# Splitting the first block by token halves, with half 1 computed among the expert gathers of half 0

## The chip, the cores and the metric

The kernel runs on one core of a Trainium2 chip. The metric is the device time of one execution in microseconds. A core has TensorE (PE, with its weight loads shown as PEld), VectorE (DVE), ScalarE (ACT), GpSimd (POOL) and SyncE (SP, which here only issues transfers). Each engine takes its instructions strictly in the order in which the program puts them into its queue.

## The reference, cut to what matters

The input is 256 tokens of width 1024. A first block adds an attention and convolution mixer and then a layer of retrieved experts; a second block (not touched by the change) follows.

```python
h = rmsnorm(x, ln_mix_g) * (1 + sc1) + sh1              # sh, sc, gt: columns of silu(c) @ w_mod + b_mod
q, kc, vc, ksl, vsl, kw, vw, gts, cb, cc, ch = jnp.split(h @ w_in, SPLIT_POINTS, axis=-1)
o_attn = nsa_mixer(...)      # 8 heads of 64: compressed blocks, all selected blocks, window, summed by gates
o_conv = cb * conv3(cc * ch) # causal, 3 taps, 512 channels
mixed = concatenate([rmsnorm(o_attn, norm_attn_g), rmsnorm(o_conv, norm_conv_g)])
x = x + gt1 * (mixed @ w_out)
h2 = rmsnorm(x, ln_ffn_g) * (1 + sc2) + sh2
x = x + gt2 * peer_ffn(h2, peer_wq, peer_keys, peer_u, peer_v)
# peer_ffn, for each token and each of 8 heads: query (2 x 64), scores against 2 x 128 keys, top 16 of each,
# top 16 of the 16 x 16 sums -> 128 experts a token, of 16384; weights g = softmax(top scores);
# act = gelu(h2 . u[e]);  out = sum over e of g * act * v[e]
```

## The kernel before

The tokens are two halves of 128, one token a partition; keys 0 to 127 serve queries of half 0, all 256 those of half 1, since attention is causal. The program is written as queues: `V(...)`, `A(...)`, `PE(...)`, `G(...)` and `SP.dma(...)` append an instruction with the ones that it waits for (`after`), so the order of the Python statements is each engine's order. All of them are issued by one helper, line 87, which is why every row of the profile bears that number. A float32 matmul is two instructions, so 8 accumulated ones count 16.

Weights stream through four slots of `W` (2 MB each, 512 columns) in the order of `plan`; `next_w` takes the next, `done_w` starts the load of the one four further on. PSUM has eight banks, taken in turn by `ps.take()`.

The order of the first block is this. (1) The projections: queries `qT`, the keys and values, the gates, then the three convolution parts (`cbT`, `ccT`, `z`, in six pieces of 32 instructions); behind each of the six, `run_step(2)` issues two of twelve `steps`: window scores, compressed blocks, their scores (`cmp_scores`), transposes (`cmp_turn`) and products (`cmp_add`). GpSimd does six weighted column sums (`mod_sum`) meanwhile. (2) Eight units of window attention, `scores(u)`, `turn_p(u)`, `pv_(u)`, four for each half (`units` holds half, group and kind); the convolution, four `conv_step(j)` over 256 columns, lies among the last. `scores` is matmuls, an add from PSUM, a row maximum (VectorE), four exponentials (ScalarE) and the weighting by sum and gate (VectorE). (3) Column sums, both norms over 256 columns, `mixT`. (4) `attn_mm(0)`, `attn_add(0)`, `queries(0)` (norm, transposes to `hT`, the projection to `qp` in two parts, key scores, transposes back to `tok2`), `attn_mm(1)`, the first two heads of `route(0)`, `attn_add(1)`, `queries(1)`.

Then the gathers begin: a loop over u in 0..255, unit u being one of the 128 chosen experts (u % 128) for each of the 128 tokens of half u // 128.

```python
for u in range(2 * P):
    n, t = fetch(a, q)          # GpSimd: indirect DMA, 128 rows of u and v, 8 KB each, into buffer n of 7
    t_dot[u] = n, V(ttr, ...)   # VectorE: dot product of the u row with tok2, one column of av
    e = combine(u)              # ScalarE: gelu, times gw, diagonal matrix dg; TensorE: dg @ v rows into PSUM
    if routes:
        advance(routes[0], 3)   # VectorE: the next 3 routing instructions
```

The seven buffers `GB` lie over `AR`, the memory of the first stages. A gather waits until TensorE has combined what was in its buffer. `route(a)` is a generator of VectorE instructions (`max`, `match_replace`, `max_index`, sums of candidates, a table lookup by `is_equal`), in groups of two, two and four heads, with one ScalarE exponential a group; `t_idx[a, h]` are the indices of a head, which the fetch of units 16h and on waits for. At u = 64 and 80 `mod_row` sums the weights of the second gate over a row; from u = 128 on the end of half 0 and the first projections of the second block lie among the gathers. Behind the loop comes the rest of the second block.

Of the kernel before, what the change touches and what calls it, by code (L numbers as in the profile page):

```python
# [112 lines left out]
def build(nc, x, cst, oh, pc, cmpw, keysT, rel, rows, ab, w_mod, w_in, w_out, wq, puv,  # L113
          w_in2, wba, wbb, wo2, out, scr):
    ctx = ExitStack()
    with ctx:
# [83 lines left out]
        s_row = dsem("s_row")  # L200
        mixT = sb("mixT", [P, 8, S])
# [13 lines left out]
        cw = ar(4288)[0:64, :]  # L215
        s_cw = dsem("s_cw")
# [73 lines left out]
        def mod_row_sum(r, n, buf, t):  # L290
            b = ps.take()
            t = PE(mm, b.t[:, :], ones, buf, start=True, stop=True, after=b.old + [t, t_in])
            o = rowb[:, r, n * 512:n * 512 + 512]
            b.free = [V(tt_, o, b.t[:, :], o, ADD, after=[t, t_row])]
            return b.free[0]

        def mod_row(r, n):
# [8 lines left out]
            b.free = [V(tt_, o, b.t[:, :], o, ADD, after=[t, t_row])]  # L306
# [9 lines left out]

        junk = sb("junk", [P, D])
# [71 lines left out]
        qT = ar(4 * S).rearrange("p (j t) -> p j t", j=4)  # L389
# [13 lines left out]
        blk = ar(2 * 32 * 30)[0:64, :].rearrange("p (v q g n) -> p v q g n", v=2, q=32, g=2)  # L403
        ksT = ar(S)
        kwT = ar(S)
        vtok = ar(2 * 2 * 128).rearrange("p (a r d) -> p a r d", a=2, r=2)
        gts = ar(48).rearrange("p (a n) -> p a n", a=2)
# [41 lines left out]
        for r in range(4):  # L449
            SP.dma(nc.sync.dma_start, s_row, rowb[:, r, :], rows[r, :].partition_broadcast(P))  # L450
# [48 lines left out]
        Pc = ar(256).rearrange("p (a h n) -> p a h n", a=2, h=8)  # L499
        cst_ = sb("cst_", [P, 2, 8, 2])  # L500
        Pb = [tok2[:, n, :] for n in range(2)]
        PT = sb("PT", [P, 2, 1024])
        pcT = ar(1024)[0:16, :].rearrange("p (n x) -> p n x", n=2)
# [43 lines left out]
        def cmp_add(a, g):  # L547
            n = 7 if a == 0 else 15
            t_c["o", g] = [add_o(a, g, vc[0:n, g * 64:g * 64 + 64], pcT[0:n, g, :], [t_c["t", a, g], t_c["v"]], False)]
# [4 lines left out]
        def scores(u):  # L554
# [6 lines left out]
            pu_ = Pb[u % 2][:, 0:4 * nk].rearrange("p (j k) -> p j k", j=4)  # L561
# [12 lines left out]
            t = V(rec, sm2[:, u, 4:8], sm2[:, u, 4:8], after=[t_e])  # L574
# [3 lines left out]
        def turn_p(u):  # L578
            a, g, r = units[u]
            nk = 128 * (a + 1)  # L580
            pu_ = Pb[u % 2][:, 0:4 * nk].rearrange("p (j k) -> p j k", j=4)
# [12 lines left out]
        def pv_(u):  # L594
            a, g, r = units[u]
            for kt in range(a + 1):
                stage[u, "O"] = add_o(a, g, vtok[:, kt, r, g * 64:g * 64 + 64], PT[:, u % 2, kt * 512:kt * 512 + 512],
                                      [stage[u, "t"][kt], t_vs, t_vw], r == 1 and kt == a)
# [35 lines left out]
        def conv_step(j):  # L634
            wc = [PV[:, V_CW + r * 4 + j:V_CW + r * 4 + j + 1] for r in range(3)]
            t = V(ts_, oc[:, j, :], z[:, j, 0:S], wc[0], None, MUL, after=[t_cv[2, j // 2], t_zz])
            t = V(stt, oc[:, j, :], z[:, j, 1:S + 1], wc[1], oc[:, j, :], MUL, ADD, after=[t])
            t = V(stt, oc[:, j, :], z[:, j, 2:S + 2], wc[2], oc[:, j, :], MUL, ADD, after=[t])
            t = V(tt_, oc[:, j, :], oc[:, j, :], cbT[:, j, :], MUL, after=[t, t_cv[0, j // 2]])
            t_oc.append((t, V(tt_, cbT[:, j, :], oc[:, j, :], oc[:, j, :], MUL, after=[t])))  # L640


        b2 = ps.take()
        t_mc = []
        t_g1 = []
        for u in range(3, 10):
            if u + 1 < 8:
                scores(u + 1)
# [1033 lines left out]
```

How the kernel before makes its waits and increments, by code:

```python
    def emit(self, eng):  # L78
        seen = {}
        for after, f, args, kw, tok, inc in self.items:
            for t in after:
                if seen.get(t.sem.name, 0) < t.value:
                    eng.wait_ge(t.sem, t.value)
                    seen[t.sem.name] = t.value
            if f is None:
                continue
            ins = f(*args, **kw)
            if inc == 16 or tok.used:
                ins.then_inc(tok.sem, inc)
```

## Time and profile before

| | |
|---|---|
| time, median of 3 runs | 1510.52 us (1508.21 to 1513.65) |
| profiled execution: time, span | 1513.2 us, 1511.3 us |
| busy: PE, DVE, ACT, POOL | 1281.6, 746.8, 477.1, 368.4 us |
| granted TensorE clock, mean | 0.948 |
| read from HBM, of it by gathers | 375.02 MB, 268.45 MB |

The times are of the slowest, here the only, core. The granted clock is the share of full speed that TensorE was given. A row names the written and the read tensor as out<-in; what stands behind an arrow in brackets is what ended an idle time. A busy TensorE is not one at its peak.

### The profile page before, as it was taken

What the parts mean: (1) busy time and instruction counts of PE and PEld (TensorE: products, weight loads), DVE (VectorE), ACT (ScalarE), POOL (GpSimd) and SP (SyncE); (2) the same over time, 40 slices, a digit from 0 to 9 for tenths busy, and PEclk for the clock granted to TensorE, in tenths of its full rate; (3) what the DMA queues carried; (4) which work ended last, traced back from release to release, by engine and by line L of the source; (5) the groups of instructions that cost most, each with busy time, mean ns of one, the idle gap of its engine ahead of it and who ended that gap; (6) DMA issues with size and microseconds to landing.
All of it is one profiled execution on the core that took longest, in us unless ns stands there. A gap on an engine that the chain in (4) does not pass through costs nothing.

```text
span 1511.3 us, 13142 instructions
## 1 busy us (share of the span) xinstructions
PE 1281.6 (85%) x4744; PEld 771.6 (51%) x4744; DVE 746.8 (49%) x1657; ACT 477.1 (32%) x1224; POOL 368.4 (24%) x285
## 2 busy tenths in 40 slices
PE   5899877887798887878889878699997789999896
PEld 1688545652233323223333322255775679999782
DVE  2313552748986696555544454511667764431212
ACT  1022220134343334344243333312785441111101
POOL 0688100134353454344334444100000000000000
PEclk9898888899999999999999999999998989999999
DMA  9775400599999999999999999645322130204130
GB/s 338 288 257 212 160 14 0 215 393 421 421 390 418 410 417 407 422 420 422 421 384 387 391 423 421 264 141 194 112 94 74 56 112 1 83 32 164 56 111 28
DMA packets 90827, 376.92 MB, mean 249 GB/s; under 512 B 6307, under 2 KB 8524, under 8 KB 57932
## 3 DMA queue, kind: packets, MB, share of 16 engines
q0 software_dynamic: 36864, 268.45, 43.3%
q1 hardware_dynamic: 52112, 103.46, 19.0%
q10 hardware_dynamic: 1788, 4.19, 0.9%
q8 instruction: 37, 0.61, 0.2%
q14 instruction: 26, 0.21, 0.0%
HBM read 375.02 MB, written 1.06 MB: 249 GB/s over the span
## 4 chain that ended last, share of the span: by engine, by line
PE 49%; DMA 21%; DVE 18%; ACT 8%; issue 2%; POOL 1%; SPq 0%; DVEq 0%; ACTq 0%; POOLq 0%
PE ps L87 49%; DMA AR<-in_puv,idx 19%; DVE AR L87 9%; DVE acc L87 3%; ACT L87 3%; DMA W<-in_w_mod 2%; ACT acc L87 2%; DVE tok L87 1%; ACT wv L87 1%; DVE RT L87 1%; ACT AR L87 1%; DVE hT L87 1%; ACT tok L87 1%; DVE junk L87 1%; POOL AR L87 1%
## 5 line engine op out<-in xcount | busy, mean ns | idle before, releaser
L87 PE MATMUL ps<-AR,acc 128*128 128x512 f32 x1024 | 500.5, 626 | 114.7 <-ACT acc L87 111.0
L87 DVE CUSTOM_DVE_ANT_0 AR<-AR,tok 128x1024 f32<-128x1024 f32 x256 | 312.6, 1223 | 219.0 <-DMA AR<-in_puv,idx 217.9
L87 POOL DMA_INDIRECT AR<-in_puv,idx x256 | 276.3, 1079 | 526.5 <-PE ps L87 390.3
L87 PEld LDWEIGHTS ps<-AR,acc 128*128 128x128 f32 x1024 | 183.8, 194 | 429.1 <-ACT acc L87 266.0
L87 PE MATMUL ps<-hT,W 128*128 128x256 f32 (+2 forms) x1504 | 323.1, 375 | 3.2 <-ACT hT L87 2.2
L87 PEld LDWEIGHTS ps<-hT,W 128*128 128x128 f32 (+1 forms) x1504 | 271.9, 198 | 46.1 <-issue 7.4
L87 ACT ACTIVATE wv<-av 128x1 f32<-128x1 f32 x256 | 51.5, 201 | 350.2 <-DVE av L87 349.9
L87 ACT ACT_TABLE_LOAD x90 | 115.5, 1283 | 16.8 <-issue 15.3
L87 ACT ACTIVATE acc<-K,wv 128x128 f32<-128x128 f32 x256 | 102.8, 402 | 8.4
L87 PE MATMUL ps<-W,hT 128*128 128x512 f32 (+3 forms) x288 | 95.2, 487 | 0.0
L87 ACT ACTIVATE wv<-wv,gw 128x1 f32<-128x1 f32 x256 | 75.4, 294 | 8.3
L87 PEld LDWEIGHTS ps<-W,hT 128*128 128x128 f32 x288 | 48.2, 191 | 45.1 <-issue 45.0
L87 ACT ACTIVATE AR<-ps 128x512 f32<-128x512 f32 (+5 forms) x53 | 24.2, 471 | 129.3 <-PE ps L87 129.3
L87 ACT ACTIVATE PT<-ps 128x512 f32<-128x512 f32 x34 | 19.8, 591 | 118.9 <-PE ps L87 118.9
L87 POOL TENSOR_TENSOR W<-W,st 128x4096 f32<-128x4096 f32 x6 | 42.2, 7026 | 61.7 <-ACT hT L87 48.5
L87 PE MATMUL ps<-AR,W 128*128 128x256 f32 x256 | 57.1, 379 | 0.0
L87 PE MATMUL ps<-K,tok 128*128 128x128 f32 x128 | 26.7, 374 | 31.8 <-DVE tok L87 31.8
L87 PEld LDWEIGHTS ps<-AR,W 128*128 128x128 f32 x256 | 48.2, 190 | 6.3
L87 PE MATMUL ps<-AR 64*64 64x30 f32 (+4 forms) x288 | 47.6, 312 | 1.0 <-DVE rowb L87 1.0
L87 PEld LDWEIGHTS ps<-AR 64*64 64x64 f32 (+2 forms) x288 | 39.0, 197 | 9.2 <-issue 5.0
L87 PEld LDWEIGHTS ps<-K,tok 128*128 128x128 f32 x128 | 21.5, 196 | 41.2 <-DVE tok L87 31.6
L87 POOL TENSOR_TENSOR W<-W 128x2048 f32<-128x2048 f32 (+1 forms) x12 | 41.7, 3473 | 0.9
(199 smaller groups left out, 1035.8 us busy)
## 6 DMA issues: line engine op xcount, KB each, us to landing
W<-in_w_in SPq DMA_DIRECT2D x25, 2048.0 KB, 7.9
W<-in_w_mod SPq DMA_DIRECT2D x12, 2048.0 KB, 16.9
W<-in_w_out SPq DMA_DIRECT2D x2, 2048.0 KB, 10.3
W<-in_wq SPq DMA_DIRECT2D x2, 2048.0 KB, 10.3
AR<-in_puv,idx POOLq DMA_INDIRECT x256, 12.7
W<-in_wba SPq DMA_DIRECT2D x2, 2048.0 KB, 7.8
W<-in_wbb SPq DMA_DIRECT2D x2, 2048.0 KB, 7.7
W<-in_wo SPq DMA_DIRECT2D x2, 2048.0 KB, 7.8
```

The costliest lines, as they stand in the source:

```text
L87: ins = f(*args, **kw)
```

## The change

The first block is computed by halves. Ahead of the first gather stands what half 0 needs: the last three `steps` and the units 4 to 7 leave the first part (unit 4 and the scores of unit 5 remain), convolution, norms and output projection are done for 128 columns (`conv_step(j, a)`, `norm_root`, `conv_mix`, `attn_root`, `attn_mix`, `attn_mm(a, n)`), the queries are projected two heads at a time (`q_norm`, `q_project`, `q_back`), and half 0 is routed for head 0 alone, then head 1, then two at a time. The rest of half 1 is the generator `half1`, one step of which is issued behind each unit from u = 1 on, on all engines. `scores` is cut into `scores` and `weigh`. As half 1 still uses the upper part of `AR`, five gather buffers turn at first, in a ring; two more join it when half 0 is fully routed. Diagonal matrices lie in `hT` until half 1 needs it. The rows of gains and gates are loaded one at a time, into tiles that serve as scratch before (keys in `R_LNF`, routing's in `R_G2`, probabilities in `R_POST`), and both `mod_row` of the second gate come when half 1 is routed.

```diff
-        for r in range(4):
-            SP.dma(nc.sync.dma_start, s_row, rowb[:, r, :], rows[r, :].partition_broadcast(P))
+        t_rows = {}
+
+        def load_row(r, after):
+            t_rows[r] = SP.dma(nc.sync.dma_start, s_rows[r], rowb[:, r, :], rows[r, :].partition_broadcast(P), after=after)
+
+        load_row(2, [])
         t_row = SP.dma(nc.sync.dma_start, s_row, abb[:, :], ab[0, :].partition_broadcast(P))
 
...
-            t = V(rec, sm2[:, u, 4:8], sm2[:, u, 4:8], after=[t_e])
+            stage[u, "x"] = t_e
+
+        def weigh(u):
+            a, g, r = units[u]
+            nk = 128 * (a + 1)
+            pu_ = Pb(u)[:, 0:4 * nk].rearrange("p (j k) -> p j k", j=4)
+            t = V(rec, sm2[:, u, 4:8], sm2[:, u, 4:8], after=[stage[u, "x"]])
             t = V(tt_, sm2[:, u, 4:8], sm2[:, u, 4:8], gts[:, a, 12 * g + 1 + r:12 * g + 12:3], MUL, after=[t, t_gt])
             stage[u, "e"] = V(tt_, pu_, pu_, sm2[:, u, 4:8].unsqueeze(2).to_broadcast([P, 4, nk]), MUL, after=[t])
 
...
-        steps += [lambda: (scores(0), compress(0)), lambda: (scores(1), compress(1)), lambda: turn_p(0), compress_k, compress_v,
-                  lambda: (scores(2), turn_p(1)), lambda: cmp_scores(0), lambda: cmp_scores(1),
+                                      [stage[u, "t"][kt], t_vs, t_vw], a == 0 and r == 1 and kt == a)
+
+        steps += [lambda: (scores(0), compress(0), weigh(0)), lambda: (scores(1), compress(1), weigh(1)), lambda: turn_p(0),
+                  compress_k, compress_v, lambda: (scores(2), turn_p(1), weigh(2)), lambda: cmp_scores(0),
                   lambda: (cmp_turn(0, 0), cmp_turn(0, 1)),
-                  lambda: (cmp_add(0, 0), cmp_add(0, 1), pv_(0), pv_(1), turn_p(2), scores(3)),
-                  lambda: (cmp_turn(1, 0), cmp_turn(1, 1)), lambda: (cmp_add(1, 0), cmp_add(1, 1))]
-
-
-        cbT = ar(4 * S).rearrange("p (j t) -> p j t", j=4)
-        ccT = ar(4 * S).rearrange("p (j t) -> p j t", j=4)
-        z = ar(4 * (S + 2)).rearrange("p (j t) -> p j t", j=4)
+                  lambda: (cmp_add(0, 0), cmp_add(0, 1), pv_(0), pv_(1), turn_p(2), scores(3), weigh(3)),
+                  ]
...
+            o = oc[:, j, c]
+            t = V(ts_, o, z[:, j, c0:c0 + P], wc[0], None, MUL, after=[t_cv[2, j // 2], t_zz])
+            t = V(stt, o, z[:, j, c0 + 1:c0 + 1 + P], wc[1], o, MUL, ADD, after=[t])
+            t = V(stt, o, z[:, j, c0 + 2:c0 + 2 + P], wc[2], o, MUL, ADD, after=[t])
+            t = V(tt_, o, o, cbT[:, j, c], MUL, after=[t, t_cv[0, j // 2]])
+            t_oc[a].append(V(tt_, cbT[:, j, c], o, o, MUL, after=[t]))
...
+        t_cn = {}
+
+        def norm_root(key, n, src, after):
+            b = ps.take()
             for j in range(4):
-                t = V(stt, mixT[:, j, a * 128:a * 128 + 128], O[a].t[:, j * 128:j * 128 + 128], PV[:, V_NA + j:V_NA + j + 1],
-                      rat[:, a * 128:a * 128 + 128], MUL, MUL, after=[e, t_os[a]] + t_mc)
+                t = PE(mm, b.t[:, 0:P], ones, src[:, j, :], start=(j == 0), stop=(j == 3), after=b.old + after)
+            e = A(act, n, b.t[:, 0:P], ACT.Sqrt, scale=1.0 / 512, bias=eps, after=[t])
+            b.free = [e]
+            t_cn[key] = e
...
+        def q_norm(a, free):
+            t_xb = norm_x(a, st[:, 12 + a:13 + a], t_x1[a], tok2, [stage[2 + 5 * a, "T"]])
+            t_hx[a], t_hx[a, "x"] = norm_T((a,), tok2, [t_xb], sc2, sh2, [t_m2] + free)
+
...
-                               start=(k == 0), stop=(k == 7), after=b.old + [t_w] + t_h)
-                e = A(act, qp[:, 4 * n:4 * n + 4, c], b.t[:, :].rearrange("p (j t) -> p j t", j=4), ACT.Copy,
-                      after=[t, t_mixfree[a]])
-                b.free = [e]
-                t_qp[a].append(e)
-                if a == 1:
-                    done_w(i, t)
-                else:
-                    kb.append(key_scores(a, n))
+            i, w, t_w = w_q[m // 2]
+            b = ps.take()
+            for j in range(2):
+                q = 2 * (m % 2) + j
+                for k in range(8):
+                    t = PE(mm, b.t[:, j * 128:j * 128 + 128], w[:, k, q * 128:q * 128 + 128], hT[:, k, c],
...
-        def key_scores(a, h4):
+        def key_scores(a, m):
             bs = [ps.take(), ps.take()]
             for p_ in range(2):
-                for q in range(4):
...
-            for h0, nh in ((0, 2), (2, 2), (4, 4)):
-                bs, t = banks[h0 // 4]
-                hp = [(h % 4, h, p_) for p_ in range(2) for h in range(h0, h0 + nh)]
+            for h0, nh in (((0, 1), (1, 1)), ((0, 2),))[a] + ((2, 2), (4, 2), (6, 2)):
+                if h0 % 2 == 0:
+                    bs, t = key_scores(a, h0 // 2)
+                    t_ks_ = t
+                t = t_ks_
...
-        ob1 = attn_mm(1)
-        routes = [route(0, kb, [stage[7, "O"]])]
+        qp = mixT
+        for j in range(4):
+            conv_step(j, 0)
+        turn_p(3)
+        pv_(2)
+        b2 = ps.take()
+        for n in range(4):
+            t_mc.append(mod_cols_sum(b2, 4 * n, *t_ms[n]))
+        sh2, sc2, t_m2 = mod_affine(b2, t_mc[3], 24, V_LNF, 16)
+        norm_root(("c", 0), nrm[:, 0, :], cbT[:, :, 0:P], t_oc[0])
+        pv_(3)
+        conv_mix(0)
+        for n in range(2):
+            t_g1.append(mod_row_sum(2, n, *t_ms[4 + n]))
+        attn_root(0)
+        attn_mix(0)
+        attn_mm(0, 0)
+        for j in range(4):
+            conv_step(j, 1)
+        attn_add(0, 0)
+        scores(4)
+        attn_mm(0, 1)
+        weigh(4)
+        attn_add(0, 1)
+        turn_p(4)
+        q_norm(0, [])
+        q_project(0, 0)
+        routes = [route(0, [])]
         while (0, 0) not in t_idx or (0, 0) not in t_gw:
             advance(routes[0], 1)
-        attn_add(1, ob1)
-        queries(1)
-
+        norm_root(("c", 1), nrm[:, 1, :], cbT[:, :, P:2 * P], t_oc[1])
+        q_back(0)
+        pv_(4)
+        q_project(0, 1)
+        scores(5)
+        conv_mix(1)
+        ring = [[n, [t_gel[0], t_gel[1], t_c["k"], t_c["v"]] + (t_mix[1] + [t_mixfree[0]] if n > 2 else [])] for n in range(5)]
+        late_t = {}
+
+        def half1():
+
+            weigh(5)
+            yield
+            turn_p(5)
+            cmp_scores(1)
+            yield
+            q_project(0, 2)
+            yield
+            pv_(5)
+            scores(6)
+            yield
+            weigh(6)
+            cmp_turn(1, 0)
+            cmp_turn(1, 1)
+            yield
+            turn_p(6)
+            load_row(1, [stage[6, "T"]])
+            cmp_add(1, 0)
+            yield
+            q_project(0, 3)
+            yield
+            scores(7)
+            yield
+            pv_(6)
+            weigh(7)
+            yield
+            turn_p(7)
+            yield
+            pv_(7)
+            cmp_add(1, 1)
+            yield
+            attn_root(1)
+            yield
+            attn_mix(1)
+            yield
+            attn_mm(1, 0)
+            yield
+            attn_mm(1, 1)
+            yield
+            attn_add(1, 0)
+            yield
+            attn_add(1, 1)
+            late_t["B"] = stage[7, "e"]
+            yield
+            late_t["dg"] = [t for f in dg_free for t in f]
+            q_norm(1, late_t["dg"])
+            yield
+            yield
+            for m in range(4):
+                q_project(1, m)
+                yield
+            q_back(1)
+            yield
 
         NG = NGB // 2
         GB = AR[:, :].rearrange("p (n d) -> p n d", n=NG)
         gsem = [dsem(f"s_g{i}") for i in range(NG)]
         av = sb("av", [P, 2, P])
         wv = sb("wv", [P, 2, P])
-        slot_free = [[t_mixfree[0], t_qp[0][-1]] for _ in range(NG)]
...
         def fetch(a, q):
-            n = (a * P + q) % NG
+            n, free = ring.pop(0)
             return n, G.dma(nc.gpsimd.indirect_dma_start, gsem[n], GB[:, n, :], None, puv,
                             bass.IndirectOffsetOnAxis(ap=idx[:, a, q:q + 1], axis=0),
-                            after=slot_free[n] + [t_idx[a, q // 16]])
+                            after=free + [t_idx[a, q // 16]])
 
         NDG = 8
...
+        h1 = half1()
         for u in range(2 * P):
             a, q = u // P, u % P
             n, t = fetch(a, q)
@@ -993,17 +1097,26 @@
                             after=[t] + t_h2[a])
             t_lastdot[a] = t_dot[u][1]
             e = combine(u)
-            if routes:
-                advance(routes[0], 3)
-                if (0, 7) in t_gw and not second:
-                    second.append(1)
-                    routes = [route(1, [key_scores(1, 0), key_scores(1, 1)], [t_idx[0, 7], t_gw[0, 7]])]
-            if u in (64, 80):
-                t_g2.append(mod_row(3, (u - 64) // 16))
+            if u >= 1:
+                advance(h1, 1)
+            advance(routes[0], 3 if u < 28 or u > 40 else 2)
+            if (0, 7) in t_gw and len(routes) == 1 and len(t_h2[1]) == 2:
+                t_eq["hold"] = [late_t["B"]]
+                eqbuf[0] = acc[:, 1, :].rearrange("p (h s j) -> p h s j", h=4, s=16)
+                ring.append([5, [stage[7, "O"], t_mix[1][-1]]])
+                ring.append([6, [stage[7, "O"], t_mix[1][-1], t_eq["last"]]])
+                routes.insert(0, route(1, [t_idx[0, 7], t_gw[0, 7]]))
+            if (1, 7) in t_gw and len(routes) == 2:
+                routes.append(None)
+                load_row(0, [t_keyfree[-1]])
+                load_row(3, [t_idx[1, 7], t_gw[1, 7]])
+                for n in range(2):
+                    t_g2.append(mod_row(3, n))
             if u == 127:
-                assert (1, 7) in t_gw
-                ahead = [x2_steps(0, e, [])]
```

## Rows read from the trace of the kernel before

**Rows 1.** Busy time by stretches: engines in us (instructions), TensorE's granted clock, DMA share, GB/s.
```profile
170.00:318.00 148.00, 116.17 (x538) 79.45 (x537) 74.87 (x199) 30.48 (x76) 6.73 (x7) 0.84 0.34 128
...
318.00:377.00 59.00, 49.33 (x104) 18.91 (x102) 41.39 (x124) 25.04 (x79) 27.31 (x26) 0.97 1.01 412
...
402.00:970.00 568.00, 471.76 (x1009) 178.29 (x1009) 340.89 (x727) 214.03 (x680) 232.77 (x214) 0.98 1.00 409
```

**Rows 2.** Timeline of GpSimd: start, duration, instruction, idle time before it and its releaser.
```profile
280.32 1.11 POOL L87 DMA_INDIRECT AR<-in_puv,idx  x1 [124.91 <-DVE hred L87]
...
321.63 0.94 POOL L87 DMA_INDIRECT AR<-in_puv,idx  x1 [0.78 <-PE ps L87]
...
376.90 0.94 POOL L87 DMA_INDIRECT AR<-in_puv,idx  x1 [1.56 <-PE ps L87]
...
489.20 0.94 POOL L87 DMA_INDIRECT AR<-in_puv,idx  x1 [11.92 <-PE ps L87]
...
957.31 0.94 POOL L87 DMA_INDIRECT AR<-in_puv,idx  x1 [1.54 <-PE ps L87]
```

**Rows 3.** Chain of waits in one unit of the gathers: start, duration, what.
```profile
611.70 1.23 DVE AR L87
...
613.98 2.00 PE ps L87 x4
```

**Rows 4.** The gathers as a group: durations in ns, first and last start, landing times.
```profile
L87 POOL DMA_INDIRECT AR<-in_puv,idx x42: 932/937/1977, 280.3 to 399.3; - x42
...
DMA to landing us min/median/max: 5.6/12.7/17.5
```

**Rows 5.** Timeline of TensorE around the compressed scores of half 0.
```profile
145.73 7.17 PE L87 MATMUL ps<-hT,W 128*128 128x256 f32 x32
154.29 1.03 PE L87 MATMUL ps<-K,AR 128*7 128x128 f32 x8 [1.38 <-DVE AR L87]
```

**Rows 6.** Chain of waits in the last unit of window scores.
```profile
200.89 1.23 DVE sm L87
202.14 2.08 ACT tok L87 x8
...
204.66 1.24 DVE tok L87
```

**Rows 7.** Timeline from the first output projection to the first indices.
```profile
229.76 16.10 PE L87 MATMUL ps<-W,mixT 128*128 128x512 f32 x32 [4.64 <-DVE modc L87]
...
245.89 0.69 DVE L87 TENSOR_TENSOR junk<-ps,rowb 128x512 f32<-128x512 f32 x1 [5.45 <-PE ps L87]
...
252.20 10.12 PE L87 MATMUL ps<-hT,W 128*128 128x128 f32 x64 [1.25 <-ACT hT L87]
...
264.64 7.41 PE L87 MATMUL ps<-hT,W 128*128 128x128 f32 x64
264.75 0.89 DVE L87 MAX8 RT<-ps 128x8 f32<-128x128 f32 x4 [13.05 <-PE ps L87]
...
279.20 0.19 DVE L87 SCALAR_TENSOR_TENSOR idx<-RT 128x32 uint32<-128x32 f32 x1
```

**Rows 8.** Groups of TensorE's instructions, 170 to 318 us: busy us, mean ns, idle before.
```profile
L87 PE MATMUL ps<-hT,W 128*128 128x128 f32 x256 | 35.0, 307 | 2.2 <-ACT hT L87 2.2
L87 PE MATMUL ps<-W,mixT 128*128 128x512 f32 x64 | 30.0, 629 | 4.6 <-DVE modc L87 4.6
L87 PE MATMUL ps<-PT,AR 128*64 128x512 f32 x20 | 12.7, 768 | 0.0
L87 PE MATMUL ps<-K,tok 128*128 128x128 f32 x52 | 10.6, 369 | 18.5 <-DVE tok L87 18.5
L87 PE MATMUL ps<-AR 64*128 64x256 f32 x32 | 9.8, 455 | 0.0
```

**Rows 9.** Timeline of ScalarE at the end of a routing group.
```profile
418.18 1.28 ACT L87 ACT_TABLE_LOAD   x1
419.48 0.26 ACT L87 ACTIVATE gw<-gw 128x64 f32<-128x64 f32 x1
```

More of the change, by code:

```diff
@@ L293, in mod_row_sum @@
             o = rowb[:, r, n * 512:n * 512 + 512]
[L294 removed]
+            b.free = [V(tt_, o, b.t[:, :], o, ADD, after=[t, t_rows[r]])]
             return b.free[0]
@@ L305, in mod_row @@
             o = rowb[:, r, n * 512:n * 512 + 512]
-            b.free = [V(tt_, o, b.t[:, :], o, ADD, after=[t, t_row])]
+            b.free = [V(tt_, o, b.t[:, :], o, ADD, after=[t, t_rows[r]])]
             return b.free[0]
@@ L659, in build @@
-        t_mix = []
-        b = ps.take()
-        for j in range(4):
-            t = PE(mm, b.t[:, 0:S], ones, cbT[:, j, :], start=(j == 0), stop=(j == 3), after=b.old + [t_oc[j][1]])
-        rcv = z[:, 0, 0:S]
-        e = A(act, rcv, b.t[:, 0:S], ACT.Sqrt, scale=1.0 / 512, bias=eps, after=[t, t_oc[3][0]])
-        b.free = [e]
-        e = V(rec, rcv, rcv, after=[e])
-        for j in range(4):
-            t_mix.append(V(stt, mixT[:, 4 + j, :], oc[:, j, :], PV[:, V_NC + j:V_NC + j + 1], rcv, MUL, MUL, after=[e] + t_mc))
@@ L669, in build @@
-        osq_ = cbT
-        t_os = []
-        for a in range(2):
-            t_os.append(A(act, osq_[:, :, a * 128:a * 128 + 128], O[a].t[:, :].rearrange("p (j t) -> p j t", j=4), ACT.Square,
-                          after=[stage[3 + 4 * a, "O"], stage[1 + 4 * a, "O"], t]))
-        b = ps.take()
-        for j in range(4):
-            t = PE(mm, b.t[:, 0:S], ones, osq_[:, j, :], start=(j == 0), stop=(j == 3), after=b.old + t_os)
-        rat = z[:, 1, 0:S]
-        e = A(act, rat, b.t[:, 0:S], ACT.Sqrt, scale=1.0 / 512, bias=eps, after=[t, t_oc[3][0]])
@@ new lines, in build, with q_project @@
+        t_hx = {}
+        t_keyfree = []
+        def q_norm(a, free):
+            t_xb = norm_x(a, st[:, 12 + a:13 + a], t_x1[a], tok2, [stage[2 + 5 * a, "T"]])
+            t_hx[a], t_hx[a, "x"] = norm_T((a,), tok2, [t_xb], sc2, sh2, [t_m2] + free)
+        def q_project(a, m):
+            c = slice(a * 128, a * 128 + 128)
+            i, w, t_w = w_q[m // 2]
+            b = ps.take()
+            for j in range(2):
+                q = 2 * (m % 2) + j
+                for k in range(8):
+                    t = PE(mm, b.t[:, j * 128:j * 128 + 128], w[:, k, q * 128:q * 128 + 128], hT[:, k, c],
+                           start=(k == 0), stop=(k == 7), after=b.old + [t_w] + t_hx[a])
+            e = A(act, qp[:, 2 * m:2 * m + 2, c], b.t[:, 0:256].rearrange("p (j t) -> p j t", j=2), ACT.Copy,
+                  after=[t, t_mixfree[a]])
+            b.free = [e]
+            t_qp[a].append(e)
+            if a == 1 and m % 2:
+                done_w(i, t)
@@ L839, in route @@
+                for u in range(nh):
+                    e = V(vidx, inx[u][:, 8:16], top[u][:, 8:16], rp[u], after=[c3[u], c4[u]])
+                    yield
+                t_sel = [e]
                 hs = slice(h0, h0 + nh)
@@ L1017, in build @@
                 rope("k", 0, t_rot["q", 0])
-        t_gfree = [f[0] for f in slot_free]
+        t_gfree = [f[0] for _, f in ring]
         t_pelast = e
```

236 lines of the change are left out of this document (117 added, 119 removed).

## The prediction

> **What bounds the kernel now.** I read three views in this order. First the busy time by stretches [rows 1]: from 318 to 377 us and from 402 to 970 us the 16 DMA engines are busy for all of the time (shares 1.01 and 1.00, 412 and 409 GB/s), while from 170 to 318 us their share is 0.34. So the kernel has a middle that is bound by bytes, the 256 gathers of 1 MB, and before it a stage in which nothing is moved and TensorE, with 116 us busy in 148, runs at a granted 0.84 of its clock. Then GpSimd's timeline [rows 2]: the first gather goes out at 280.3 us, the last at 957.3. In the steady part a gather follows each 2.485 us (0.94 of GpSimd and 1.55 of its wait for TensorE at 376.9 us); the 42nd goes out at 399.3 us [rows 4], so the one at 376.9 is nine paces before it, the 33rd. Last the chain of waits [rows 3]: one unit is a gather that lands, 1.23 us of VectorE (the dot product, "dot" below, 1.3 with reading its sum), then 1.05 us until TensorE starts at 613.98, in which ScalarE has three instructions (gelu, weight, diagonal matrix; 0.95 without the crossing, "G"), and 2.0 us of TensorE ("C"), after which the buffer is free. A landing takes 5.6 us with nothing else under way, 12.7 in the median [rows 4]: seven buffers hold the pace because the rest waits in the queue of transfers.
>
> So the end moves by one thing: by how much later or earlier a given unit is combined, since from then on 2.485 us per gather are due in both kernels. The number to compare with: when the 33rd gather is issued at 376.9 us, units 0 to 25 are combined.
>
> **Start of the gathers.** The change needs only head 0 of half 0 before the first gather.
> - In the projections, the compressed scores and their transposes of half 0 now stand directly behind one another in TensorE's queue. Between them lies a chain of VectorE that today ends at 154.3 us; TensorE does a projection of 7.2 us meanwhile and then idles 1.38 us for it [rows 5]. That projection now comes after it: 6 us later, and the projections end at 176.4 instead of 170.2.
> - Today it is 24 us from the last weighed probabilities (205.9, [rows 6]) to the first output projection (229.8, [rows 7]): column and row sums, both norms, both over 256 columns. Now the norms have 128 columns, and the convolution's 4 x 5 VectorE instructions go ahead at half width: I take 16 us (bounds 12 and 24), to 192.
> - Output projection of half 0: 30.0 us for 64 instructions [rows 8], so 7.5 for 16, twice, 15; between them scores of unit 4, 2.45 (9.8/32 x 8): 209.5.
> - Adds, norm and transposes: today 245.9 to 252.2 [rows 7], 6.3 us, and 1 more for a table load and the copies of unit 4 before the root: 216.8. Queries of two heads, 32 instructions of 35.0/256: 4.4. Evacuation 0.5 and key scores 1: 222.7.
> - Routing of two heads took from 264.75 us to the indices at 279.4 [rows 7], 14.6; of one head, 8.3 (half, and 1 for instructions that don't shrink). First gather at **231 us**, against 280.3. Unit 0 is combined after landing (5.6 us), routing's weights, three VectorE instructions of scores of unit 5 and the mix of the second convolution half: at 241; unit 1 begins at 243.5.
>
> **Half 1 among the gathers.** Here lies the price. A step is issued behind unit u on all engines, and unit u+1 behind the step, each engine in order. Step and unit can overlap only where no engine waits in between. R, three routing instructions, is 1.0 us (14.6 us over 47). Three kinds of step:
> - ScalarE takes the result (queries, turns). C + step + copy + G, since G of the next unit stands behind the copy. Queries: 2.0 + 4.4 + 0.5 + 0.95 = 7.85, six times, **47.1**. Turns of probabilities (8 transposes of 10.6/52, 1.6, [rows 8]): 5.2, twice, with one of them a small product: **10.4**. Turn of compressed ones 4.6, back-transposes 5.25, root 5.65: **15.5**.
> - VectorE takes it and ScalarE follows. Scores: C 2.0, matmuls 2.45, last add 0.7 (as the add of the same shape at 245.89, [rows 7]), maximum 1.2, exponentials 2.1 [rows 6], then the table load 1.28 and G 0.95: 10.7. Units 4 and 8, the first with a value product of 2.5 (12.7/20 x 4) ahead: 13.2 + 10.7 = **23.9**. Compressed scores with the turn of unit 5: 10.4. Norm and transposes: 8.2. Together **18.6**.
> - Nothing waits in between. Output projection 2.0 + 7.5, twice: **19.0**. Value products 4.5 and 5.3. VectorE alone (weights 1.6, mix 2, adds 1.4, each with R and a dot): 3.9, 4.3, 3.7, 3.7; one empty step 2.5. Together **27.9**.
>
> Sum of the 24 steps: 47.1 + 10.4 + 15.5 + 23.9 + 18.6 + 19.0 + 27.9 = 162.4 us. Routing's exponential falls in it twice, with a table out and back and VectorE waiting, 3 us each: 168. Unit 25 begins at 243.5 + 168 = 411.5 and is done at 414, against 376.9: **37 us later**. Everything rests on this: TensorE would be busy for some 120 of these 170 us, and the DMA engines carry 31 gathers and 8 MB of weights, some 95 us. What was gained by starting 49 us earlier is spent because the DMA engines idle while half 1 is computed; today they are full from 280 us on, with weights and seven gathers, while TensorE does half 1.
>
> The table load is priced from the row: 1.28 us, and the next instruction starts 0.02 us behind it [rows 9]. The Trainium skill (ScalarE: Activation LUTs, What ACT_TABLE_LOAD costs) counts a drain of 1380 ns as well, 2.66 us for a switch, and advises doing all work of one set first. Here this rule speaks against the change, which puts seven switches out and back among the gelus; by its figure 14 x 1.38 = 19 us would be added, an estimate from that page. The trace does not show such a gap, so the sum leaves it out.
>
> **After unit 25.** Until half 0 is fully routed, near unit 62, only five buffers turn. From below: a landing of 5.6 us + 4.5 of work, over 5, is 2.0 us, under 2.485, no loss. From above: 12.7 + 4.5 over 5 is 3.4 us, 37 units x 0.95 = 35 us. The nearest row is the low one, because the queue shortens by itself; but with 2.3 us of slack any stall is felt, so 4 us. Two rows of 512 KB are loaded among the gathers: 1 MB at 409 GB/s, 2.5 us, of which the idle stretch takes part: 1.5. The two sums over modulation weights move from units 64 and 80 to about 124, together, and the vector add then waits for its row to land. One such sum today lets GpSimd idle 11.92 us [rows 2] with landings queued for about that long; two in a row would leave some 6 us uncovered, but two weight loads of 2 MB follow and fill it: 0 (bounds 0 and 6). Other edits (bank by bank releases, scratch tiles moved, keys and rows in other tiles) are costed at nothing: they lie in the idle parts of SP and DMA before 231 us. The tail behind the gathers is the same code.
>
> Sum: 37 + 4 + 1.5 = 42.5 us. The profiled execution took 1513.2 us at a span of 1511.3, so 1555.7 for it; it lay 2.7 above the median of the runs, so **1553** by the median.
>
> **Rivals.**
> - *Packed (faster).* If the engines slide past each other, only TensorE's work counts from 241 us on: 26 units at 1.72 us (0.94 + 0.78, the pace at 323 us with matmuls back to back, [rows 2]) and about 60 us of half 1 (six queries 22, from 7.41 us for 64 instructions, [rows 7]; the two projections 14; an estimated 24 for the rest of [rows 8] at full clock): 346, 31 us before 376.9. With 5.5 lost later: 1485. The point where it turns: if the round trips cost less than 31 us in 24 steps, 1.3 us each. For it: the steps are spaced so that weights and turns come a step later. Against it: G alone is 0.95 and always stands behind a copy. Chance 0.22, between 1485 and 1506.
> - *Starved ring.* The steps cost what I say, and the five buffers lose 10 to 35 us more, or the drain of the page exists: 1570 to 1590. Chance 0.10.
> - *Even.* Round trips cost half, start and loss cancel: 1510 within 4.5 us. Chance 0.07.
> - *Likeliest,* 0.61: 1525 to 1572.
>
> **Range and chances.** Below 1497 lies about a tenth, the better part of the packed case; above 1580 less than a tenth: 1497 to 1580. The likeliest case alone has 1525 to 1572. A measurement of this kernel tells changes of about 0.3%, 4.5 us. Faster 0.23, same 0.07, slower 0.70.
>
> **What would show it.** First gather near 231 us (a step late in the first part if over 240). DMA share from there to the end of half 1 about 0.6, not 1.0. The 31st gather is issued near 414 us; near 350 the packed case is true. TensorE waits for ScalarE's diagonal matrices, 40 to 50 us in that stretch, with its granted clock below 0.9. Gaps between gathers of about 2.5 us from unit 26 on; 3 and more to unit 62 means a starved ring. I am wrong if ScalarE's part of a unit does not stand behind the step's copies, or if the stage ahead of 231 us is longer by what I took off the norms.

## The result and the profile after

The changed kernel took 1564.5 us (median of 4 runs, 1561.7 to 1568.7), the kernel before 1512.1 beside it (4 runs): a ratio of 1.035, 95% interval 1.032 to 1.039. The forecast was 1553, within 1497 to 1580. The profiled execution after took 1561.7 us at a span of 1559.9, so its span is 48.6 us longer. The medians lie 52.4 us apart.

The stretches of the kernel after, in the columns of [rows 1]:

```profile
170.00:238.00 68.00, 56.88 (x244) 38.36 (x243) 39.92 (x119) 14.81 (x34) 0.00 (x0) 0.85 0.19 70
238.00:405.00 167.00, 117.44 (x444) 65.16 (x444) 77.17 (x205) 61.71 (x149) 33.25 (x30) 0.88 0.66 238
405.00:662.00 257.00, 193.74 (x425) 72.62 (x424) 194.73 (x571) 100.22 (x301) 114.17 (x97) 0.95 0.95 383
662.00:739.00 77.00, 62.76 (x128) 24.07 (x128) 40.76 (x71) 28.87 (x79) 27.53 (x25) 0.96 0.98 391
739.00:1010.00 271.00, 229.81 (x496) 88.46 (x496) 134.97 (x230) 96.93 (x328) 108.91 (x106) 0.99 1.00 408
```

The second row is the price. Where 31 gathers lie among half 1, TensorE works for 117 us of 167 at a clock of 0.88, and the DMA share is 0.66, no engine full. In the kernel before the share is 1.01 from 318 us on [rows 1]. From 739 us on both kernels are alike. GpSimd's timeline, to be read against [rows 2], with the first gather, the 31st, the 61st, the one behind the two row sums and the last:

```profile
238.05 1.11 POOL L87 DMA_INDIRECT AR<-in_puv,idx  x1 [82.00 <-DVE hred L87]
...
405.37 1.82 POOL L87 DMA_INDIRECT AR<-in_puv,idx  x1 [3.51 <-PE ps L87]
...
493.89 0.94 POOL L87 DMA_INDIRECT AR<-in_puv,idx  x1 [1.55 <-PE ps L87]
...
698.86 0.94 POOL L87 DMA_INDIRECT AR<-in_puv,idx  x1 [19.24 <-PE ps L87]
...
1008.18 0.93 POOL L87 DMA_INDIRECT AR<-in_puv,idx  x1 [1.56 <-PE ps L87]
```

The first goes out 42.2 us earlier than before, the last 50.9 us later. With five buffers the 31st (405.37) says that unit 25 is combined, as the 33rd at 376.90 does before: 28.5 us later. The 61st (493.89) waits for unit 55; the gather that does so before, the 63rd, goes out at 454.69: 39.2 later. The 127th waits for unit 119 in both, 661.9 against 626.2: 35.7 later; the 151st 738.7 against 687.1: 51.7. The 63rd, the 127th and the 151st of the kernel before:

```profile
454.69 0.94 POOL L87 DMA_INDIRECT AR<-in_puv,idx  x1 [1.89 <-PE ps L87]
...
626.18 0.94 POOL L87 DMA_INDIRECT AR<-in_puv,idx  x1 [1.55 <-PE ps L87]
...
687.05 0.94 POOL L87 DMA_INDIRECT AR<-in_puv,idx  x1 [1.36 <-PE ps L87]
```

What TensorE waited for, from 244 to 405 us (sum, times, longest):

```profile
PE ps L87 <- ACT hT L87: 36.9, 12, 6.5
PE ps L87 <- ACT acc L87: 10.9, 6, 4.1
```

`hT` and `acc` hold the diagonal matrices: 47.8 us, of which 6.5 are the wait for unit 0, ahead of any step. One such wait in full, from the timeline of all engines:

```profile
296.09 1.98 PE L87 MATMUL ps<-AR,hT 128*128 128x512 f32 x4 [0.59 <-ACT hT L87]
...
297.91 3.73 PE L87 MATMUL ps<-hT,W 128*128 128x128 f32 x32
...
301.68 0.38 ACT L87 ACTIVATE mixT<-ps 128x256 f32<-128x256 f32 x1 [5.64 <-PE ps L87]
301.96 0.19 ACT L87 ACTIVATE wv<-av 128x1 f32<-128x1 f32 x1
302.19 0.30 ACT L87 ACTIVATE wv<-wv,gw 128x1 f32<-128x1 f32 x1
302.52 0.40 ACT L87 ACTIVATE hT<-K,wv 128x128 f32<-128x128 f32 x1
302.94 1.28 ACT L87 ACT_TABLE_LOAD   x1
302.97 1.55 PE L87 MATMUL ps<-AR,hT 128*128 128x512 f32 x3 [1.33 <-ACT hT L87]
```

TensorE does a unit's product (296.09) and then a step of half 1, the queries (297.91). ScalarE must copy these out (301.68), since the copy stands ahead of the next unit's gelu in its queue; only then come gelu, weight and diagonal matrix, and TensorE starts the next product at 302.97, 6.88 us after the last. It worked for 5.6 of them. The unit's dot product was done: the gelu at 301.96 waits for nothing. Such a stretch, in which TensorE waits for ScalarE and ScalarE has itself waited for TensorE, is called a round trip below.

### The profile page after: what moved, and what is told of

Read it like the earlier page. It is cut to its first block, busy times and chain, and to the rows that moved or that the text cites. A ratio compares the mean times of both kernels' runs of the same rounds, so it can differ in the third digit from the quotient of the medians.

```text
span 1559.9 us, 13266 instructions
## 1 busy us (share of the span) xinstructions
PE 1285.0 (82%) x4760; PEld 773.4 (50%) x4760; DVE 755.0 (48%) x1728; ACT 503.4 (32%) x1252; POOL 375.9 (24%) x285
## 4 chain that ended last, share of the span: by engine, by line
PE 51%; DMA 18%; DVE 17%; ACT 10%; issue 2%; POOL 1%; SPq 0%; DVEq 0%; ACTq 0%
PE ps L87 51%; DMA AR<-in_puv,idx 16%; DVE AR L87 9%; ACT L87 4%; DVE acc L87 2%; DMA W<-in_w_mod 2%; ACT wv L87 2%; ACT acc L87 2%; DVE RT L87 1%; POOL AR L87 1%; ACT AR L87 1%; DVE hT L87 1%; DVE tok L87 1%; DVE rowb L87 1%; ACT rowb L87 1%
## 5 line engine op out<-in xcount | busy, mean ns | idle before, releaser
L87 PE MATMUL ps<-AR,acc 128*128 128x512 f32 x948 | 467.2, 630 | 132.6 <-ACT acc L87 131.9
L87 POOL DMA_INDIRECT AR<-in_puv,idx x256 | 283.9, 1109 | 569.2 <-PE ps L87 463.2
L87 DVE CUSTOM_DVE_ANT_0 AR<-AR,tok 128x1024 f32<-128x1024 f32 x256 | 311.7, 1220 | 177.6 <-DMA AR<-in_puv,idx 176.4
L87 PEld LDWEIGHTS ps<-AR,acc 128*128 128x128 f32 x948 | 171.5, 195 | 418.1 <-ACT acc L87 268.1
L87 ACT ACT_TABLE_LOAD x109 | 139.8, 1283 | 17.3 <-issue 15.4
L87 ACT ACTIVATE acc<-K,wv 128x128 f32<-128x128 f32 x237 | 95.2, 402 | 7.8
L87 PE MATMUL ps<-AR,hT 128*128 128x512 f32 x76 | 44.0, 716 | 36.9 <-ACT hT L87 36.9
L87 PEld LDWEIGHTS ps<-AR,hT 128*128 128x128 f32 x76 | 15.5, 221 | 58.2 <-ACT hT L87 42.3
## 6 DMA issues: line engine op xcount, KB each, us to landing
AR<-in_puv,idx POOLq DMA_INDIRECT x256, 10.6
```

The costliest lines, as they stand in the source:

```text
L87: ins = f(*args, **kw)
```

## The experiments

All times are medians, ratios are to the kernel before run beside them (1510.3 to 1512.1 us). The table gives how much later than before a gather was issued in the profiled execution, in us, from GpSimd's timeline of each, with a minus where it was earlier; those before are at 371.9, 449.4, 626.2, 687.1 and 957.3. In the first two columns a version of the change has fewer buffers than before, so there they are for comparing versions with one another. "Lag" stands for one thing only, the product of a unit issued one unit later than before; each "and" adds to the version above it.

| kernel | 31st | 61st | 127th | 151st | last | time | ratio (95%) |
|---|---|---|---|---|---|---|---|
| after | +33.4 | +44.4 | +35.7 | +51.7 | +50.9 | 1564.5 | 1.035 (1.032 to 1.039) |
| sums apart | +31.9 | +42.5 | +54.1 | +53.8 | +53.7 | 1567.7 | 1.038 (1.036 to 1.041) |
| half 1 ahead | +39.9 | +48.4 | +41.3 | +54.7 | +55.1 | 1567.1 | 1.036 (1.033 to 1.040) |
| every second unit | -2.9 | +44.1 | +36.2 | +49.0 | +50.5 | 1561.1 | 1.034 (1.031 to 1.037) |
| weights first | -0.3 | +10.1 | +3.0 | +15.4 | +15.9 | 1524.7 | 1.009 (1.006 to 1.011) |
| and sixth buffer | -2.4 | +1.3 | -7.3 | +4.7 | +5.1 | 1518.4 | 1.006 (1.004 to 1.007) |
| and sums later | -2.5 | +1.5 | -7.4 | +6.7 | +3.7 | 1517.4 | 1.004 (1.003 to 1.006) |
| and late lag | -1.4 | +3.7 | -6.7 | +1.0 | -1.5 | 1508.0 | 0.998 (0.997 to 1.000) |
| and lag all through | -4.2 | -5.1 | -16.1 | -9.0 | -11.2 | 1502.2 | 0.995 (0.994 to 0.997) |
| late lag, every second | -26.5 | -0.3 | -10.5 | -2.8 | -4.2 | 1507.5 | 0.998 (0.997 to 1.000) |
| before, one head | -0.8 | +6.4 | +2.1 | +1.5 | +2.5 | 1516.2 | 1.004 (1.003 to 1.006) |
| before, lag | -2.6 | -4.1 | -2.7 | -3.9 | -9.0 | 1502.1 | 0.995 (0.994 to 0.997) |

**Sums apart.** The two row sums of the second gate go back among the gathers (80 and 96), with the scratch of routing's half 1 in another tile.

```diff
...
+                load_row(3, [t_idx[0, 7], t_gw[0, 7]])
...
-                for n in range(2):
-                    t_g2.append(mod_row(3, n))
+            if u in (80, 96):
+                t_g2.append(mod_row(3, (u - 80) // 16))
```

> The changed kernel with its two row sums of the second gate taken apart again: half 1 is routed with scratch in the free probability tile, so row 3 is loaded near unit 62 and the sums stand behind units 80 and 96. Theory: between the gathers 126 and 132 of the changed kernel 16 us were lost, because 14 us of TensorE in one piece are more than the landings queued behind seven buffers cover; one sum of 7 us is covered. 16 us less than the changed kernel: 1548. Rival: the lag was only waiting to show there and comes back elsewhere: 1560 or more.

Measured 1567.7. Each lone sum costs as well. The kernel to compare with is the one after, which has no sum there (the kernel before has its second at the same unit). This version is 0.9 us ahead of it at the 85th gather, 12.8 behind at the 91st and 18.4 at the 127th, behind both sums; at the 151st, behind the pair of the kernel after, 2.2 are left. So two sums apart cost 19.3 us, weights included, and the pair costs the kernel after 16.0 from the 127th to the 151st: it is not the pair that is uncovered, and the miss refutes that theory. GpSimd's timeline behind the first sum:

```profile
577.40 2.02 POOL L87 DMA_INDIRECT AR<-in_puv,idx  x1 [11.98 <-PE ps L87]
579.73 1.91 POOL L87 DMA_INDIRECT AR<-in_puv,idx  x1 [0.30 <-PE ps L87]
581.94 1.89 POOL L87 DMA_INDIRECT AR<-in_puv,idx  x1 [0.30 <-issue]
```

And VectorE's in the same stretch, its dot products alone:

```profile
577.40 1.21 DVE L87 CUSTOM_DVE_ANT_0 AR<-AR,tok 128x1024 f32<-128x1024 f32 x1
...
579.60 1.22 DVE L87 CUSTOM_DVE_ANT_0 AR<-AR,tok 128x1024 f32<-128x1024 f32 x1
...
581.80 1.22 DVE L87 CUSTOM_DVE_ANT_0 AR<-AR,tok 128x1024 f32<-128x1024 f32 x1
```

These issues, which meet a dot product, take 1.9 to 2.0 us where 0.94 is usual. With the 0.3 between them GpSimd then has a pace of 2.2 us against the 2.485 of the bytes, so a queue of transfers that has run short fills slowly. That this is why a stall is not made up for is argued; no run changed it.

**Half 1 ahead.** All of half 1 in one piece ahead of unit 0, the first five gathers under way beside it: `for _ in h1: pass` ahead of the loop.

> The changed kernel with all 24 steps of half 1 issued in one piece ahead of the first unit; only the first five gathers are in flight meanwhile. Theory that the round trips between unit and step are the price: without them half 1 takes about 85 us, the first unit is combined near 325 us and unit 25, then bound by the transfers, near 388 instead of 405: 1547. Rival that only the sum of TensorE's work counts: interleaving is free and uses the gathers' time, so taking it out makes unit 25 later, 415 or more: 1575.

Measured 1567.1, between the two cases, so a miss for both. The 5th gather goes out at 248.8, the 6th at 342.3, the 31st at 411.8: half 1 by itself keeps the gathers back for some 93 us, and the 25 units behind it take 69.5. The 31st of the kernel after is at 405.4. So interleaving as written saves only 6 us at the 31st gather against one after the other, and nothing that can be told in the times.

**Every second unit.** A step only behind odd units: `if u >= 1 and u % 2`.

> The changed kernel with a step of half 1 behind every second unit instead of every one. Theory: the units between steps find their gathers landed and go at TensorE's pace, about 1.9 us instead of 2.485, so 24 of them give back 14 us: 1550. Rival, five buffers are too few and each long step starves the ring whatever its spacing: 1564 or more.

Measured 1561.1. The 31st gather comes 36 us earlier than in the kernel after, but the 58th at 484.0 against 485.1, and the time is the same within the noise. A miss again: ordinary units between the steps save nothing by then. The round trips may only be spread over more units, or five buffers starve whatever the spacing, as the expectation's rival says; this run does not separate the two.

**Weights first.** The three instructions of ScalarE stay ahead of the step, the product comes one unit later, for u < 26 except 18 (where half 1 takes the tile of the diagonal matrices back).

`weight` is the ScalarE part of the former `combine`, and `combine` what is left, the product:

```diff
...
-            e = combine(u)
+            weight(u)
+            behind.append(u)
+            while len(behind) > (u < 26 and u != 18):
+                e = combine(behind.pop(0))
             if u >= 1:
                 advance(h1, 1)
```

> The changed kernel in which, up to unit 25, a unit's dot product and its three ScalarE instructions are issued before the step of half 1 as now, but its product on TensorE one unit later, behind that step. So the next unit's diagonal matrix no longer waits behind the copy of a step's result. Theory that this order is what costs: about 1.3 us a step, more at the two scores, 30 us in all: 1535. Rival, VectorE's waits for the steps' matmuls or the lower clock are what costs: less than 8 us, 1557 or more.

Measured 1524.7, 10 below what was expected: 40 us of the 52 are gone by one change of order. ScalarE's queue is the same as in the kernel after; it is TensorE that asks for a diagonal matrix one step later, when it no longer has the step's copy ahead of it. Its busy times from 238 to 372 us:

```profile
238.00:372.00 134.00, 112.91 (x444) 63.95 (x444) 78.61 (x210) 63.55 (x150) 31.70 (x31) 0.90 0.77 286
```

What TensorE waited for in it:

```profile
PE ps L87 <- ACT hT L87: 13.8, 4, 6.5
PE ps L87 <- ACT acc L87: 4.1, 1, 4.1
PE ps L87 <- ACT AR L87: 2.5, 1, 2.5
```

The same 444 instructions now take 134 us where they took 167. TensorE waits 17.9 us for diagonal matrices instead of 47.8 (6.5 of each for unit 0), and is busy for 112.9 us instead of 117.4, at a clock of 0.90 instead of 0.88: so most of the 33 us are waits. The end of this stretch on TensorE's timeline:

```profile
365.41 1.45 PE L87 MATMUL ps<-AR,acc 128*128 128x512 f32 x3
366.70 1.04 PE L87 MATMUL ps<-K,hT 128*128 128x128 f32 x8
367.57 3.73 PE L87 MATMUL ps<-AR,acc 128*128 128x512 f32 x8
```

Product and step follow one another with no idle time.

**And sixth buffer.** The sixth buffer joins the ring when half 1 is done, not when half 0 is routed.

```diff
+            if len(t_h2[1]) == 2 and not late_t.get("five"):
+                late_t["five"] = True
+                ring.append([5, [stage[7, "O"], t_mix[1][-1]]])
...
-                ring.append([5, [stage[7, "O"], t_mix[1][-1]]])
```

> The fourth experiment (weights of a unit ahead of the step of half 1) and a sixth gather buffer that joins as soon as half 1 is done, near unit 26, not near 62. In the fourth, unit 25 was 5 us ahead of the kernel before and unit 55 some 5 us behind it. Theory of a starved ring: five buffers lose these 10 us between 26 and 62, a sixth gives at least half of it back: 1518 or less. Rival: five hold the pace and routing's load on VectorE loses it: no change, 1525.

Measured 1518.4: the 61st gather at 450.8 against 459.6. Five buffers cost some 9 us from the end of half 1 to the end of routing; these return 11 at the last gather of the profiled execution, 6 in the medians, 5 by the ratios. The landings are longer with six, 10.2 us in the median against 7.7 (405 to 494 us of each), as more of them are under way.

**And sums later.** The two sums come 5 and 14 units behind the end of routing.

```diff
-                for n in range(2):
-                    t_g2.append(mod_row(3, n))
+                late_t["u"] = u
+            if "u" in late_t and u - late_t["u"] in (5, 14):
+                t_g2.append(mod_row(3, len(t_g2)))
...
```

> The fifth experiment, and the two row sums of the second gate apart, 5 and 14 units behind the end of routing instead of together at its end, so that the row has landed before VectorE comes to it. After subtracting the bytes of two weight blocks and two rows, 12.5 us, the pair had cost some 5 us of idle transfers. Theory that one piece of 14 us is too long to cover: 5 us less than the fifth. Rival, that each stall of TensorE costs by itself, as the first experiment has it: no change or 3 more.

Measured 1517.4, the same. Place and spacing of the sums are worth nothing that a measurement tells here.

**And late lag.** The product one unit behind also from unit 64 on, except 127 and 255.

> The sixth experiment, and from unit 64 on too the product of a unit one unit behind its weights. Theory that also routing's exponentials, with two table loads, hold up TensorE: 3 to 5 us less. Rival: a buffer is now held one unit longer, seven allow a landing of only 10.4 us, and nothing is gained or some us are lost.

Measured 1508.0, 9 us less than without, about twice what was expected: the first version of the change that is not slower. GpSimd stood idle for 5.1, 5.0 and 6.1 us ahead of the 86th, 102nd and 118th gathers in the version without, and for 0.8, 0.7 and 0.6 us here.

**Before, one head.** The kernel before with the first two heads of routing as two groups: the first gather goes out at 273.5 instead of 280.3.

> The kernel before with only its first routing group cut into two of one head each, so that its first gather goes out some 6 us earlier. Theory that the start of the gathers is not what sets the end, since TensorE combines unit 0 no earlier and the transfers of weights fill the time: within 3 us of the kernel before. Rival, that every microsecond of earlier start is one off the end: 6 less.

Measured 1516.2 (ratio 1.004, 1.003 to 1.006): not the 6 us less of the rival, but 5 us more, outside the 3 us of the expectation. The 10th gather is 1.3 us earlier, the last 2.5 later. An earlier start gives nothing here; the edit also adds a routing group with its exponential (92 table loads for 90), and the 5 us may be the price of that, which was not tested apart.

**Lag all through, every second unit, and before with lag.** The first is the kernel with late lag, with the lag in units 26 to 63 as well:

```diff
-            while len(behind) > ((u < 26 and u != 18) or (u >= 64 and u not in (127, 255))):
+            while len(behind) > (u not in (18, 127, 255)):
```

> The kernel with first and late lag, six buffers and the later sums, with the lag also in units 26 to 63. If the stalls that remain there are round trips behind routing's exponentials, 2 to 4 us less than the same kernel without it: about 1505. If buffers are what is short there, a unit held one turn longer costs more than it gives: 1508 or up to 8 us above.

The second has the lag to unit 50 and from 64 on, and a step behind every second unit:

> The kernel with first and late lag, six buffers and the later sums, with a step of half 1 behind every second unit and the lag to unit 50. If the gathers between the steps only shift work, as with every second step in the kernel after, the 60th gather goes out at the same time and the end is the same within 4.5 us. If TensorE's slack between steps is used, half 1 costs less and the time is 5 to 15 us lower.

The third is the kernel before with nothing but the lag:

```diff
-            e = combine(u)
+            weight(u)
+            behind.append(u)
+            while len(behind) > (u not in (127, 255)):
+                e = combine(behind.pop(0))
```

> The kernel before, with each unit's product issued one unit behind its diagonal matrix, except for units 127 and 255. It separates what the order alone is worth, without the change. If the lag helps wherever VectorE or ScalarE hold a unit up (routing's exponentials, the row sums), it gains here as it did late in the kernel with seven buffers: 5 to 9 us, about 1503. If the lag is worth something only where foreign steps stand between the units, the kernel before has none of these before unit 128 and stays at 1511 within 4.5 us. The 126th gather, at 626 us in the kernel before, shows which.

Measured 1502.2, 1507.5 and 1502.1. The lag in units 26 to 63 gives 4 to 6 us more (by the ratios, by the medians), somewhat above the forecast. The every-second version ends as the kernel with late lag does (1508.0), as expected if the gathers between the steps only shift work. The kernel before with lag meets its first case, 1503. It is as fast as the best version of the change, though it starts its gathers 40 us later. The last gather of the version with the change, on GpSimd's timeline:

```profile
946.13 0.94 POOL L87 DMA_INDIRECT AR<-in_puv,idx  x1 [1.55 <-PE ps L87]
```

And of the kernel before with the lag:

```profile
948.26 0.94 POOL L87 DMA_INDIRECT AR<-in_puv,idx  x1 [1.55 <-PE ps L87]
```

The every-second version has its 31st gather at 345.4, 26.5 us ahead of before, and gives most of it back while the rest of half 1 is done: 4.9 us ahead at the 45th, 6.8 at the 49th, 2.6 at the 55th, 4.2 at the last.

## Why the prediction was right, and where its terms were off

The side, the mechanism and its place were as forecast: the order on ScalarE makes each step a round trip. TensorE waited 47.8 us for diagonal matrices, 41.3 of them at steps (forecast 40 to 50), the DMA share was 0.66 (0.6), the clock 0.88 (below 0.9). Weights first shows it: its only change is that TensorE no longer asks for something behind the step's copy, and 40 us go. How near the total came is in part luck, since its terms erred both ways:

- **Start.** First gather at 238.05, forecast 231. The projections ended at 176.7 (176.4); the step that failed is the one after them, column sums and norms: the first output projection began at 196.6 instead of 192, so halving the columns saved 4 us of 24, not 8. The rest, 2.5, lies in what follows.
- **Half 1.** Unit 0 was combined near 248, not 241, and unit 25 at 405.4, not 414: +28.5 instead of +37. The price of most steps was too high. The last four steps of queries follow each other on TensorE in 6.88 us, against 7.85 (timeline of TensorE):

```profile
379.85 3.73 PE L87 MATMUL ps<-hT,W 128*128 128x128 f32 x32
384.91 1.98 PE L87 MATMUL ps<-AR,acc 128*128 128x512 f32 x4 [1.32 <-ACT acc L87]
386.73 3.73 PE L87 MATMUL ps<-hT,W 128*128 128x128 f32 x32
391.79 1.98 PE L87 MATMUL ps<-AR,acc 128*128 128x512 f32 x4 [1.32 <-ACT acc L87]
```

  These 32 instructions take 3.73 us here, at a granted clock of 1.00 (372 to 396 us). The 4.4 came from a group [rows 8] in a stretch whose clock was 0.84. The first of the six steps took 4.89 (262 to 290 us, clock 0.75), the other five 3.73, so the six cost 23.5 us of matmuls, not 26.3. From unit 0 to unit 25 it took 157.6 us, against 173 in the sum. TensorE's timeline takes it apart from the product of unit 1 (251.3) to that of unit 25 (403.1), 151.8 us against 168: steps of queries 2.9 less, those in which nothing waits 6.6 less, scores and norm 2.6 less, turns and root 1.5 more; and the 5.6 for routing's exponentials do not come on top of these, they are in them.
- **The ring.** +10.7 us from unit 25 to unit 55 (28.5 to 39.2), forecast 4 and a row's 1.5. The busy times of that stretch, after and before:

```profile
405.40:493.90 88.50, 64.68 (x136) 24.27 (x136) 60.66 (x177) 31.00 (x97) 31.70 (x31) 0.92 0.88 347
376.90:454.70 77.80, 64.32 (x152) 24.11 (x152) 68.53 (x185) 29.15 (x92) 36.09 (x31) 0.96 0.99 406
```

  The DMA share is 0.88 instead of 0.99: the 0.12 that are missing of 88.5 us are 10.6. The sixth buffer gives 9 back. The low bound took a landing of 5.6 us. The issues of the stretch from 405 to 494 us say 7.7 in the median:

```profile
AR<-in_puv,idx POOLq DMA_INDIRECT x31, 7.7
```

  7.7 + 4.5 over 5 is 2.44 us, so next to nothing was left of the slack of 2.3 us that the 4 us rested on. That the waits for routing's exponentials were felt in full for this reason is argued. From the 31st gather to the 61st a gather took 2.95 us, just under the 3 that the prediction names as the sign of a starved ring.
- **Rows and sums.** From unit 55 to the 151st gather +12.5 more (39.2 to 51.7), forecast 0. Both kernels do their two sums, with 4 MB of weights, inside this stretch. The kernel after moves 97.65 MB in its 244.8 us, the kernel before 96.62 MB in its 232.35: 2.5 us are the two rows of 512 KB, the other 10 a lower rate (399 GB/s for 416). Part of that are round trips at routing's exponentials for half 1: GpSimd stands idle 4.2, 5.8 and 5.9 us ahead of the 86th, 102nd and 118th gathers, and late lag takes these idle times away, and with them 5.2 us at the last gather, 9 in the medians. Spacing and place of the sums are not the cause: sums apart gave +2.8, sums later -1.4 us at the last gather. What the rest is stays open.
- **The tail** gave back 3.1 us (51.7 to the 48.6 of the spans); it was costed at nothing.

28.5 + 10.7 + 12.5 - 3.1 = 48.6. Errors of opposite sign, 8.5 too much in half 1, 17.7 too little behind it (23.2 for 5.5) and 3.1 too much in the tail, left the sum 6 us low in the span. The forecast lay 11.5 below the median; the other 5.4 or so come from its step to medians: the profiled execution before lay 2.7 above the median that it used, the one after 2.8 below its own.

**The rivals.** *Packed* was worked out for engines that slide past each other, with unit 25 done at 346. Weights first has it done at 371.6: packing saves 34 us, half of the 68 between that rival and the sum, and with all else mended the kernel gets to 1502, not 1485. *Starved ring* was true in kind, but small: the stretch lost 10.7 us where the sum had 5.5, so 5 more and not 10 to 35. Its second half, the drain of the page (ScalarE: Activation LUTs, What ACT_TABLE_LOAD costs, in the Trainium skill), is not in the trace: ScalarE's timeline has, in a step of scores of the kernel after:

```profile
282.70 1.28 ACT L87 ACT_TABLE_LOAD   x1
...
283.99 0.20 ACT L87 ACTIVATE wv<-av 128x1 f32<-128x1 f32 x1
```

The measurement decides here: 0.01 us from the end of the load to the next instruction. Behind none of the 55 loads of this execution where the next instruction waits for nothing is the gap over 0.10 us.

**What the change is worth with its cause mended.** The idea was a gift of 42 us at the start. With order and buffers put right, unit 25 is done at 367.7 (31st gather, five buffers), against 374.3 in the kernel before with the lag (33rd, seven buffers). That lead of 6.6 us is 2.1 at the last gather, and the times are the same. Three kernels say so from three sides: an earlier start with one more routing group (one head) gives nothing, half the steps (late lag, every second) gives 26.5 us of which some 5 are left 14 gathers later, and lag all through equals before with lag. The busy times of lag all through, ahead of its first gather and then with half 1, in the columns of [rows 1]:

```profile
170.00:238.00 68.00, 54.53 (x241) 36.18 (x239) 39.78 (x118) 15.71 (x35) 0.85 (x1) 0.87 0.19 70
238.00:368.00 130.00, 111.36 (x442) 63.67 (x443) 76.36 (x201) 59.91 (x146) 30.63 (x31) 0.90 0.78 289
```

TensorE has 166 us of work in 198. The kernel before does its half 1 with the weights of the second block and seven gathers loading beside it, and is full of bytes from there. That TensorE's own work is the floor of this stretch fits these rows; no run took work away from it, so that is argued and not shown.

## What to carry to other kernels

Where work is spliced into a pipelined loop, look at the engine that both copies out the spliced work's results and feeds the loop's next product. If that product asks for something behind the copy, each step becomes a round trip. Put the loop's small instructions ahead of the copy and issue the product one turn later (40 of 52 us here). Before moving work under transfers, ask which engine would be full when both are packed; here an earlier start was worth nothing, and the likely reason, argued and not shown, is that TensorE's work is the sum either way. Try the remedy on the old kernel too: here the lag alone made the old order 0.5% faster (ratio 0.995, 0.9936 to 0.9968).

## What the runs showed of the hardware

GpSimd's issue of an indirect DMA usually takes 0.94 us, and up to 2.0 where a VectorE instruction with two inputs in SBUF, the dot product of 1.2 us, is under way when it starts. In the kernel after, from 250 to 994 us, 40 issues start with over 0.6 us of a dot product still to go, and 34 of them take over 1.5 us; 117 start together with a dot product or up to 0.94 us ahead of one, and 116 of them take 1.26 or less. So the one that starts first is what matters. This agrees with the Trainium skill (SBUF — State Buffer, Who interferes with whom), by which a VectorE instruction with two SBUF inputs contends with a GpSimd instruction that reads SBUF, and the port pair that they share is an exclusive lock. The same section infers that such an instruction does not hold up the generation of descriptors; the issues of these indirect DMAs are held up.

The granted clock in half 1 rose from 0.88 to 0.90 when the same work was packed into 134 us.
